# One layout and one product form changed in a two-block kernel: xT stored by chunk, and 24 weight tiles multiplied as 512 + 256 columns a chunk with VectorE adding the two sums

## The reference, cut to what matters

```python
def hybrid_mixer(u, w_in, conv_w, conv_b, w_rg_a, b_rg_a, w_rg_i, b_rg_i, lru_lambda, ...):
    proj = jnp.einsum("bsd,dc->bsc", u, w_in)          # 1024 -> 7 x 1024 columns
    q, k, v, x_lru, g_lru, gate_attn, gate_lru = jnp.split(proj, list(SPLITS), axis=-1)
    cos, sin = rope_tables(s)
    qh = partial_rope(to_heads(q), cos, sin)           # rotates 32 of each head's 128 features
    kh = partial_rope(to_heads(k), cos, sin)
    ...
    xc = causal_depthwise_conv(x_lru, conv_w, conv_b)  # xc = bias + sum of 4 taps w[j] * shifted x_lru
    hl = rg_lru(xc, w_rg_a, b_rg_a, w_rg_i, b_rg_i, lru_lambda)
```

## Time and profile before

| what | before |
|---|---|
| median of 3 timed runs | 1190.28 us |
| the profiled execution: its span, first to last instruction | 1188.1 us |
| TensorE busy | 1058.3 us |
| GpSimd busy | 691.4 us |
| VectorE busy | 677.0 us |
| ScalarE busy | 531.9 us |

### The profile page before, as it was taken

One profiled execution on the slowest core, in us unless ns is written; L12 is line 12 of the kernel. 1 busy time (PEld: TensorE's weight loads), 2 busy tenths in 40 slices (PEclk: granted clock), 3 DMA queues, 4 the chain that ended last, 5 costly groups with the idle time before them and its releaser, 6 DMA issues.

```text
span 1188.1 us, 14710 instructions
## 1 busy us (share of the span) xinstructions
PE 1058.3 (89%) x4782; PEld 715.6 (60%) x4782; DVE 677.0 (57%) x1467; ACT 531.9 (45%) x1305; POOL 691.4 (58%) x431
## 2 busy tenths in 40 slices
PE   9998998988898877877777778999999999999998
PEld 7874554544454322332232234998999997888886
DVE  2577888878586576784674446424454553621323
ACT  5865434433422322323223225546666436544544
POOL 5734544344444433443344342985797986988885
PEclk9999999999999999899999999999999999999999
DMA  7779999999999999999999997773444554656552
GB/s 254 266 259 422 407 421 420 421 421 421 422 420 421 422 421 421 395 423 422 421 421 421 418 421 307 242 230 115 159 159 160 181 178 157 210 180 198 191 182 101
DMA packets 66530, 372.26 MB, mean 313 GB/s; under 512 B 7672, under 2 KB 8800, under 8 KB 33632
## 3 DMA queue, kind: packets, MB, share of 16 engines
q0 software_dynamic: 37152, 268.45, 54.6%
q1 hardware_dynamic: 26800, 97.02, 24.6%
q10 hardware_dynamic: 2512, 5.94, 1.5%
HBM read 369.80 MB, written 1.06 MB: 312 GB/s over the span
## 4 chain that ended last, share of the span: by engine, by line
PE 54%; DMA 29%; DVE 7%; ACT 4%; issue 4%; POOL 2%; ACTq 0%; DVEq 0%; POOLq 0%
DMA arena<-in_peer_uv,idx_all 29%; PE ps L1971 12%; PE ps L1656 10%; PE ps L1658 10%; PE ps L1657 10%; PE ps L1680 5%; DVE arena L1425 3%; PE ps L1681 3%; DVE arena L1556 1%; PE ps L2032 1%; POOL arena L470 1%; ACT prob L783 1%; ACT wts L777 1%; POOL w_hl L454 1%; ACT gel L770 1%
## 5 line engine op out<-in xcount | busy, mean ns | idle before, releaser
L1971 PE MATMUL ps<-arena,prob 128*128 128x512 f32 x1024 | 478.5, 614 | 114.7 <-ACT prob L783 114.6
L470 POOL DMA_INDIRECT arena<-in_peer_uv,idx_all x254 | 280.1, 1103 | 371.3 <-PE ps L1971 333.4
L454 POOL TENSOR_TENSOR w_hl<-ring,w_hl 128x1024 fp32r<-128x1024 f32 x146 | 367.2, 2530 | 103.4 <-ACT w_hl L561 102.4
L1971 PEld LDWEIGHTS ps<-arena,prob 128*128 128x128 f32 x1024 | 189.5, 194 | 388.0 <-ACT prob L783 194.1
L1425 DVE CUSTOM_DVE_ANT_0 arena<-arena,xn 128x1024 f32<-128x1024 f32 x256 | 312.0, 1224 | 189.1 <-DMA arena<-in_peer_uv,idx_all 186.5
L770 ACT ACTIVATE gel<-acts 128x2 f32<-128x2 f32 (+1 forms) x130 | 26.5, 204 | 399.7 <-DVE acts L1425 399.2
L561 ACT ACTIVATE w_hl<-ring 128x1024 fp32r<-128x1024 f32 x157 | 165.4, 1059 | 82.1 <-PE ps L1658 81.4
L1656 PE MATMUL ps<-xT,w_hl 128*128 128x256 f32 x568 | 163.4, 288 | 1.7 <-DVE xT L1063 0.6
L1658 PE MATMUL ps<-xT,w_hl 128*128 128x256 f32 x568 | 160.7, 283 | 0.0
L1657 PE MATMUL ps<-xT,w_hl 128*128 128x256 f32 x568 | 160.7, 283 | 0.0
L1656 PEld LDWEIGHTS ps<-xT,w_hl 128*128 128x128 f32 x568 | 108.9, 192 | 3.4 <-POOL w_hl L454 1.9
(11 more groups left out here) (324 smaller groups left out, 1327.4 us busy)
## 6 DMA issues: line engine op xcount, KB each, us to landing
ring<-in_weights SPq DMA_DIRECT2D x174, 512.0 KB, 3.3
arena<-in_peer_uv,idx_all POOLq DMA_INDIRECT x254, 12.5
held<-in_weights SPq DMA_DIRECT2D x4, 512.0 KB, 6.0
arena<-in_rg_weights ACTq DMA_DIRECT2D x1, 2048.0 KB, 8.6
bias<-rel_scratch ACTq DMA_DIRECT2D x1, 1024.0 KB, 6.4
arena<-in_subkeys SPq DMA_DIRECT2D x1, 1024.0 KB, 7.8
out_x<-x ACTq DMA_DIRECT2D x4, 256.0 KB, 2.1
arena<-in_band SPq DMA_DIRECT2D x1, 768.0 KB, 6.7
```

What stands on the lines that cost most here:

```text
L454: pool.tensor_tensor(pair[:, 1], raw(n), pair[:, 0].bitcast(F32), ALU.subtract).then_inc(w_lo, 1)
L470: pool.indirect_dma_start(uv_slot(n), None, A["peer_uv"], bass.IndirectOffsetOnAxis(idx_all[:, h, c:c + 1], 0))\
L1971: j = pe.matmul(banks(2 + 2 * t + half), diag[:, n % GRING, :], uv_slot(n)[:, D + half * 512:D + (half + 1) * 512], start=(h == 0 and c % ...
```

## The change

Four things change together.

- `xT` is stored with the two halves of a chunk side by side, so that hi and lo of a chunk are 512 columns in one run.
- Tiles 0 to 23 are multiplied by `halves_product`, two matmuls a chunk (512 and 256 columns) instead of three of 256. The bank then holds two partial sums, `main_of(f)` and `rest_of(f)`.
- ScalarE copies the main sum out (for tiles 0 to 7 to a new place `x_lru`, no longer with tap and bias). VectorE adds the rest in place (`add_rest`), and this addition (`halves_sum`) frees the bank.
- For tiles 0 to 7 the first tap becomes a `tensor_scalar` on VectorE, and the three others read `x_lru` in SBUF instead of PSUM. The 16 additions of tiles 8 to 23 stand on VectorE ahead of both rotations.

```diff
-        xT = sb("xT", [P, 2, NC_, SEQ], F32R)
+        xT = sb("xT", [P, NC_, 2, SEQ], F32R)[:].rearrange("p c k s -> p k c s")
...
@@ scalar
-                act.activation(xc[:, m, :], banks((F_X2 + m) % 2)[:, 0:SEQ], ACT.Identity,
-                               scale=cols[:, C_CW + 24 + m:C_CW + 25 + m],
-                               bias=cols[:, C_CB + m:C_CB + m + 1]).then_inc(proj_evac, 1)
+                act.activation(x_lru[:, m, :], main_of(F_X2 + m), ACT.Identity).then_inc(proj_evac, 1)
...
-                act.wait_ge(proj_evac, F_QK2 + 8 * n + 8)
+                act.wait_ge(halves_sum, 8 + 8 * n + 8)
...
                 if f in (1, 4):
+                    act.wait_ge(halves_sum, 24)
                     swap_half(1, f // 4)
@@ vector
+            def add_rest(f, to):
+
+                dve.wait_ge(proj_evac, f + 1)
+                dve.tensor_tensor(to, rest_of(f), to, ALU.add).then_inc(halves_sum, 1)
+
             for m in range(8):
+                add_rest(F_X2 + m, x_lru[:, m, :])
+                dve.wait_ge(halves_sum, m + 1)
+                dve.tensor_scalar(xc[:, m, :], x_lru[:, m, :], cols[:, C_CW + 24 + m:C_CW + 25 + m],
+                                  cols[:, C_CB + m:C_CB + m + 1], ALU.mult, ALU.add).then_inc(tap_zero, 1)
                 for back in (1, 2, 3):
                     if back == 1:
-                        dve.wait_ge(proj_evac, F_X2 + m + 1)
+                        dve.wait_ge(tap_zero, m + 1)
                     else:
                         dve.wait_ge(conv_step, 3 * m + back - 1)
-                    dve.scalar_tensor_tensor(out=xc[:, m, back:], in0=banks((F_X2 + m) % 2)[:, 0:SEQ - back],
+                    dve.scalar_tensor_tensor(out=xc[:, m, back:], in0=x_lru[:, m, 0:SEQ - back],
                                              scalar=cols[:, C_CW + 8 * (3 - back) + m:C_CW + 8 * (3 - back) + m + 1],
                                              in1=xc[:, m, back:], op0=ALU.mult, op1=ALU.add).then_inc(conv_step, 1)
 
+            for m in range(16):
+                add_rest(F_QK2 + m, projT[:, m, :])
@@ tensor
+            def halves_product(f, n, wait, fresh=lambda c: None):
+
+                w = weight(n)
+                wait()
+                for c in range(NC_):
+                    fresh(c)
+                    pe.matmul(banks(f % 2), w[:, 0, c, :], xT[:, :, c, :].rearrange("p k s -> p (k s)"),
+                              start=c == 0, stop=False)
+                    i = pe.matmul(rest_of(f), w[:, 1, c, :], xT[:, 0, c, :], start=False, stop=c == NC_ - 1)
+                i.then_inc(w_used, 1)
...
-            for m in range(8):
-                f = F_X2 + m
-                product(f, W_X2 + m, fresh_xTc(2) if m == 0 else xTc,
-                        evacuated(f) if m < 2 else (lambda: pe.wait_ge(conv_step, 3 * (m - 1))))
-            for m in range(16):
-                f = F_QK2 + m
-                product(f, W_QK2 + m, xTc,
-                        evacuated(f) if m >= 2 else (lambda: pe.wait_ge(conv_step, 3 * (8 + m - 1))))
+            for m in range(24):
+                halves_product(F_X2 + m, W_X2 + m,
+                               evacuated(F_X2 + m) if m < 2 else (lambda: pe.wait_ge(halves_sum, m - 1)),
+                               fresh_xT(2) if m == 0 else (lambda c: None))
 
             pe.wait_ge(conv_step, 24)
+            pe.wait_ge(halves_sum, 24)
             pe.wait_ge(rgw_ld, 16)
```

More of the change, by code:

```diff
@@ L230, in build @@
         swapped = [projT[0:ROT, 16:24, :], prob[0:ROT, 0:2048].rearrange("p (h s) -> p h s", h=8)]
+        x_lru = projT[:, 32:40, :]
         a_buf = projT[:, 16:24, :]
@@ L324, in build @@
         hid_main, hid_sum = sem("hid_main"), sem("hid_sum")
+        halves_sum, tap_zero = sem("halves_sum"), sem("tap_zero")
         def tr_banks(k, t):
@@ L368, in up_rest, with main_of, rest_of @@
             return banks(m % 4)[:, SEQ:2 * SEQ]
+        def main_of(f):
+            return banks(f % 2)[:, 0:SEQ]
+        def rest_of(f):
+            return banks(f % 2)[:, SEQ:2 * SEQ]
         def scores_of(h):
@@ L1685, in _, with fresh_xT @@
             xTc = lambda c: parts(xT, c, slice(None))
-            def fresh_xTc(k):
+            def fresh_xT(k):
                 def chunk(c):
-                    if c % 2 == 0:
+                    if c % 4 == 0:
                         pe.wait_ge(xT_dve, 4 * k + 2 + c // 4 + 1)
-                    return xTc(c)
                 return chunk
```

## The result

The changed kernel takes 1204.0 us (median of 5 runs, 1202.47 to 1208.94); the kernel before took 1190.37 in the same comparison. The ratio on record is 1.0127, with a 95% interval of 1.0113 to 1.0140 (the two medians alone give 1.0115, inside it). The forecast was 1203, in a range of 1195 to 1208.

The account below looks back on a forecast made before the run. TensorE was taken to bound the kernel before, VectorE's turns with splits the changed tiles 3 to 10. Terms of +14.3, -1.5, -0.6 and +1.1 gave +13.3: span 1201.4, plus 2.2 gives 1203.6, stated 1203, range 1195 to 1208.

Parts of the forecast that it names:

- What bounds, and the exclusion: TensorE bounds tiles 0 to 22; VectorE operations within SBUF and GpSimd splits exclude each other for their whole length.
- The matmuls: Two matmuls a chunk instead of three, tiles 0 to 23: gain 0.11 us a tile, 2.6 in all.
- The first stretch: Up to tile 3, each SBUF operation waits behind one back-to-back split; tile 3 starts 5.1 us late.
- The period: Tiles 3 to 10: VectorE sets the pace, one split a tile, 4.2 us each (3.4 to 4.5).
- The clock: In a slower rival, the clock falls in TensorE's gaps of 1.4 us a tile; rival's chance 0.07.
- Wait ahead of the gates: After tile 23, the gates wait for evacuation, addition and three handovers of about 0.1: +1.1 us.
- The late split at 809.41: In the q and k tiles, TensorE's wait for a split delayed by the rotation goes: -0.6 us.
- The first rotation: Rotation of q, moved behind all additions, starts with the gates, takes 6.9 to 11.5 us and stays hidden.
- The sum: Whole kernel: +14.3 at tile 10, -1.5 matmuls, -0.6 split wait, +1.1 ahead of the gates, in all +13.3 us.
- The turns cost nothing: Faster rival: VectorE and GpSimd fit beside each other, TensorE stays the bound; -2.1 us, 1188.2; chance 0.08.
- Only the first stretch is lost: No-change rival: `tensor_scalar` not excluded, 2.5 us lost at the start, near nothing a tile after; +0.4, 1190.7; chance 0.05.

Follow-up runs that it names:

- The PSUM taps with two waits: Changed kernel with taps reading PSUM, x_lru tiles in four banks, the gates' first two products each waiting for one addition: 1187.20 us, ratio 0.9987.
- with the clock held up: Changed kernel with 9, 4 and 9 dummy matmuls ahead of TensorE's waits of tiles 3, 6 and 9: 1203.66 us, ratio 1.0120.
- one tap an addition: Changed kernel with ScalarE making the first tap and VectorE's other 24 taps dealt out behind its additions, mostly one each: 1189.51 us, ratio 0.9998.
- four banks: Changed kernel with four banks for the x_lru tiles and nothing else, taps still reading SBUF: 1206.02 us, ratio 1.0147.
- the additions first: Changed kernel with VectorE's 24 additions in tile order and the 32 convolution operations dealt out behind them: 1195.23 us, ratio 1.0062.

## Why the prediction was right

**What bounds, and the exclusion.** Right, and shown from both sides: without splits the SBUF taps are short (0.48 us, 1186.7 us in all), without SBUF taps the splits do no harm (1188.4 us).

**The matmuls.** Forecast 0.11 us a tile, measured 0.05 in this execution: tiles 10 to 23 of the changed kernel start 2.83 us apart. The step that was off is the row chosen: the pairs of the earlier trace rows come from the MLP's first turn, at 0.346, and later turns of the same kernel run at 0.353. The PSUM taps with two waits ran at 0.346 throughout. So the gain is 0.05 to 0.11 a tile, 1.3 to 2.6 us for 24, and the forecast took the upper end as its value.

**The first stretch.** Forecast: tile 3 late by 5.1 us. Measured: it starts 13.69 us into the stage, against 3.22 + 2 x 2.88 = 8.98 by the prediction's reckoning (9.08 in the trace of before): 4.6 to 4.7 late, by the steps described, each tap behind one split.

**The period.** Forecast 4.2 us, bounds 3.4 and 4.5. From tile 3 to tile 10 passed 45.36 - 13.69 = 31.7 us, 4.5 a tile; with the clock held up, 4.4. The terms that were mis-sized are the operations themselves: 0.41 for the `tensor_scalar` (0.25 taken) and 0.48 for a tap (0.38 taken, 0.43 called the most, though the earlier trace rows had 483 ns for such an operation with one input in PSUM). With them the forecast's own sum is 2.37 + 0.41 + 3 x 0.48 + 0.42 = 4.6, less the 0.2 by which a tap that waited is shorter. Its shape was wrong too: the waits came in three blocks of 2.7 to 4.9 us, not one of 1.4 a tile. While TensorE stands still GpSimd runs dry and VectorE catches up a tile or two; then the splits come in a bunch again. What the prediction left out there is the clock: with it held up, tiles 4 to 8 came evenly with waits of 0.9 to 1.4 us, as forecast, and at nearly the same 4.4 a tile. (The upper bound of its sum, 1208.3, takes 1.0 us off behind tile 10 where its own bounds, no gain of the matmuls and 0.6 for the split, give 0.6.)

**The clock.** It was named only as part of a rival with a chance of 0.07 and no price of its own. It did happen, and cost 0.6 to 1.5 us.

**The small terms.** Wait ahead of the gates: 1.0 us (forecast 1.1, with three handovers of 0.1 that no row showed; only their sum with the two operations is measured). The late split at 809.41 went. The first rotation started when the gates did and delayed nothing; VectorE is busy 13.1 of the 14.0 us of that window.

**The sum.** Tile 10 late by 16.1 (45.36 us into the stage against 29.24; forecast 14.3), then -0.7 (-1.5), -0.6 (-0.6) and +1.0 (+1.1): +15.8 in the stage, of which 1.7 us is offset by differences outside, above all where tile 0 starts, which differs by 1.8 us among the other kernels too. The nearness of 1203 to 1204.0 is therefore in part luck: the stage lost 2.5 us more than forecast.

**The rivals.** *The turns cost nothing* falls for this order, but nearly holds as a limit: with one excluded operation an addition the time is that of the kernel before (0.9998), with 1.0 us of waits for additions. *Only the first stretch is lost* falls: the `tensor_scalar` is excluded as well. It took 1.74, 2.00 and up to 2.5 us.

## What to carry to other kernels

Where VectorE works beside GpSimd, look at where each VectorE operand lies, not only at how long the operation is: an operation with two inputs in SBUF, or a float32 `tensor_scalar` within it, waits until a running GpSimd instruction that reads SBUF has ended (here 0.48 us became up to 2.6 beside splits of 2.4). Moving an input from PSUM to SBUF to free a bank early can lose far more than the bank was worth (here 15.8 us in the stage). If it can't be avoided, put at most one such operation between two operations that another engine waits for, and never several in a chain ahead of one.

## What the runs showed of the hardware that was not expected

- A pair of 512 and 256 columns has two paces at full clock, 0.346 and 0.353 us. Within the stage it changed between them only at a wait: with one tap an addition, tiles start 2.77 us apart up to tile 10, 2.83 behind the waits there, and 2.77 again behind the wait of tile 19. With no wait between tiles it kept 2.77 through the stage in one kernel and 2.83 in another. What sets it stays open; over 24 tiles it is 1.3 us, as much as the product form gains at the slower pace, so differences of about 1 us between single profiles of this stage say little.
- A float32 `tensor_scalar` of 256 columns takes 0.41 us within SBUF and 0.54 from PSUM; the `scalar_tensor_tensor` takes 0.48 from either.
- TensorE's clock fell to half around each idle stretch of 2.4 to 7.6 us between tiles (4.7, 2.4 and 4.6 in the changed kernel, 6.1 and 7.6 with four banks). It did not in the kernel with the shorter fillers, where five idle stretches of at most 1.4 us lay between tiles. In between it went either way: it fell after 1.85 us ahead of the gates (one tap an addition), and did not after 2.04 and 1.85 us with the additions first.
